# Second mixer's softmax steps: row maxima ahead of finished heads, evacuation of transposes ahead of squares and conversions, first output products inside the last steps

## The reference

```python
q = (rms_norm(cq, qa_g) @ w_uq).reshape(B, S, MLA_HEADS, MLA_QK)          # 6 heads of 128 + 64
kv = (rms_norm(ckv, kva_g) @ w_ukv).reshape(B, S, MLA_HEADS, MLA_NOPE + MLA_VDIM)
...
q = rms_norm(q, qn_g)
k = rms_norm(k, kn_g)
... # rotary on the last 64 of q and k; then, per block of 128 queries:
s = jnp.einsum('bqhd,bkhd->bhqk', qi, k).astype(jnp.float32) * scale
s = jnp.where(kpos[None, :] <= qpos[:, None], s, -jnp.inf)
p = jax.nn.softmax(s, axis=-1)
return jnp.einsum('bhqk,bkhd->bqhd', p.astype(v.dtype), v)
...
m = memory_attention(z[..., -MEM_W:], rms_norm(mem, mem_norm_g[layer]), w_mem_kv[layer],
                     mem_q_norm_g[layer], mem_k_norm_g[layer])            # 4 heads, 256 memory tokens
x = x + jnp.concatenate([y, m], axis=-1) @ w_out[layer]                   # y: 6 heads of 128, m: 256
x = x + conv_ffn(rms_norm(x, ffn_norm_g[layer]), w_up[layer], ...)
```

## Time and profile before

| | us |
|---|---|
| median of 3 runs (lowest, highest) | 1961.98 (1960.8, 1971.39) |
| the profiled execution | 1967.27 |
| its span | 1965.3 |
| TensorE busy | 1861.8 (95%) |
| VectorE busy | 901.7 (46%) |
| ScalarE busy | 737.6 (38%) |
| GpSimd busy | 725.4 (37%) |
| mean granted TensorE clock | 0.971 |

### The profile page before, as it was taken

The page is one execution under the profiler, slowest core; times in us unless marked ns, Lnnn a source line. Parts: engine busy times, 40 slices in busy tenths (PEclk is TensorE's granted clock), DMA queues, the critical chain, the costliest instruction groups (busy, mean ns, idle before and its releaser), DMA issues.

```text
span 1965.3 us, 24503 instructions
## 1 busy us (share of the span) xinstructions
PE 1861.8 (95%) x9553; PEld 1496.6 (76%) x9553; DVE 901.7 (46%) x1293; ACT 737.6 (38%) x977; POOL 725.4 (37%) x226
## 2 busy tenths in 40 slices
PE   7999979999999999988899999998899999999998
PEld 5799754788888887565788888886787778878876
DVE  5245754356554116555355555104516734413453
ACT  4142143355545224453345455223213542221323
POOL 2253820334443444221144444343324434343321
PEclk8989996999999999999999999999999999999999
DMA  6632110222222232110122222223131112322121
GB/s 258 253 107 87 44 44 1 72 100 88 104 101 79 88 97 95 42 65 22 43 88 104 99 93 87 88 88 121 65 84 45 55 65 86 120 88 105 65 86 43
DMA packets 28663, 170.30 MB, mean 87 GB/s; under 512 B 2992, under 2 KB 5296, under 8 KB 12208
## 3 DMA queue, kind: packets, MB, share of 16 engines
q1 hardware_dynamic: 25200, 151.20, 22.3%
q10 hardware_dynamic: 3392, 18.09, 2.8%
HBM read 167.18 MB, written 2.10 MB: 86 GB/s over the span
## 4 chain that ended last, share of the span: by engine, by line
PE 66%; issue 17%; DVE 7%; POOL 7%; ACT 3%; DMA 0%; POOLq 0%; ACTq 0%; DVEq 0%
PE ps L390 40%; PE ps L714 11%; POOL wlo L1035 5%; POOL hk L1061 1%; PE ps L408 1%; PE ps L409 1%; PE ps L410 1%; DVE scr L2063 1%; PE ps L956 1%; PE ps L805 1%; PE ps L966 1%; PE ps L939 1%; PE ps L967 1%; PE ps L968 1%; PE ps L687 1%
## 5 line engine op out<-in xcount | busy, mean ns | idle before, releaser
L1035 POOL TENSOR_TENSOR wlo<-wraw,whi 128x2048 fp32r<-128x2048 f32 (+3 forms) x153 | 650.1, 4249 | 1112.0 <-ACT whi L1151 1094.1
L390 PE MATMUL ps<-hh,whi 128*128 128x512 f32 x1344 | 527.4, 392 | 2.3 <-DVE sig L2233 1.6
L390 PE MATMUL ps<-hl,whi 128*128 128x512 f32 x1344 | 523.1, 389 | 0.0
L390 PE MATMUL ps<-hh,wlo 128*128 128x512 f32 x1344 | 523.1, 389 | 0.0
L1151 ACT ACTIVATE whi<-wraw 128x2048 fp32r<-128x2048 f32 (+3 forms) x149 | 265.0, 1779 | 416.0 <-PE ps L390 326.1
L390 PEld LDWEIGHTS ps<-hh,whi 128*128 128x128 f32 x1344 | 252.3, 188 | 58.9 <-issue 3.6
L390 PEld LDWEIGHTS ps<-hh,wlo 128*128 128x128 f32 x1344 | 252.3, 188 | 53.0
L390 PEld LDWEIGHTS ps<-hl,whi 128*128 128x128 f32 x1344 | 252.4, 188 | 52.5 <-issue 1.2
L1900 DVE SCALAR_TENSOR_TENSOR scr<-ps,vec,scr 128x510 f32<-128x510 f32 (+1 forms) x176 | 120.2, 744 | 93.2 <-ACT scr L1344 93.2
L714 PE MATMUL ps<-gh,whi 128*128 128x512 f32 x352 | 137.1, 390 | 1.3 <-DVE gl L1915 1.3
L714 PE MATMUL ps<-gh,wlo 128*128 128x512 f32 x352 | 137.0, 389 | 0.0
(11 more groups left out here) (432 smaller groups left out, 2857.0 us busy)
## 6 DMA issues: line engine op xcount, KB each, us to landing
wraw<-in_w SPq DMA_DIRECT2D x63, 1024.0 KB, 4.9
wraw<-in_w0b SPq DMA_DIRECT2D x26, 1024.0 KB, 4.8
wraw<-in_w1o SPq DMA_DIRECT2D x26, 1024.0 KB, 4.9
wraw<-in_wd SPq DMA_DIRECT2D x32, 704.0 KB, 4.1
ada<-in_wada ACTq DMA_DIRECT2D x12, 1024.0 KB, 7.1
xtok<-in_x SPq DMA_DIRECT2D x4, 512.0 KB, 7.9
out<-ytok SPq DMA_DIRECT2D x2, 1024.0 KB, 4.2
wraw<-in_w SPq DMA_DIRECT2D x3, 576.0 KB, 3.9
```

The source lines that it names most:

```text
L390: last = mm(o, l, r, start=(k == 0 and n == 0), stop=(k == K - 1 and n == 2))
L1035: nc.gpsimd.tensor_tensor(wlo[:, s % 2, 0:wd], wraw[:, s % 2, 0:wd], whi[:, s % 2, 0:wd].bitcast(F32), ALU.subtract).then_inc(lo_ready, 1)
```

## The change

On VectorE the row maxima of a pass come ahead of the finished head. Both heads of a pair are copied together, ahead of the normalisation, and the low part of the second one is taken in the next pass. On ScalarE the squares and conversions move behind the evacuation of the transposes; the values' evacuation and job 8 stay ahead of it. TensorE does 36 of the 48 products of output slot 0 in passes 17 to 20, between transposes and scores, and 12 products of slot 1 before the last 12 of slot 0. Slot 1 no longer waits for slot 0's addition. Slots 2 and 3 are as they were. GpSimd and SyncE have the lists that they had.

```diff
@@ TensorE
+            Y_ORDER = (6, 7, 0, 1, 2, 3, 4, 5)
+            def out_part(s, j0, j1):
+                for j in range(j0, j1):
+                    k = Y_ORDER[j]
+                    pe.wait_ge(split_done, Q_Y1 + j + 1)
+                    for b in range(2):
+                        o, w_ = ps[:, 2 * (s % 2) + b, :], wv(s % 2, 256, off=b * P)
+                        mm(o, w_(0, k), y_act(0, k), start=(j == 0), stop=False)
+                        mm(o, w_(0, k), y_act(1, k), start=False, stop=False)
+                        last = mm(o, w_(1, k), y_act(0, k), start=False, stop=(j == 7))
+                return last
...
+                if n >= 17:
+                    if n == 17:
+                        pe.wait_ge(m_ev, taken(2, 11))
+                        pe.wait_ge(lo_ready, S_O1 + 1)
+                    out_part(S_O1, *((0, 2), (2, 4), (4, 5), (5, 6))[n - 17])
                 if n < 19:
                     pe.wait_ge(g_ex, 2 * n + 2)
...
                     step_pv(n - 1).then_inc(g_pv, 1)
-            out_slots(S_O1, Q_Y1, act=lambda a, k: (oh1, ol1)[a][:, k, :] if k < 6 else (ohm, olm)[a][:, k - 6, :],
-                      order=(6, 7, 0, 1, 2, 3, 4, 5))
+            pe.wait_ge(g_ex, 40)
+            pe.wait_ge(lo_ready, S_O1 + 2)
+            out_part(S_O1 + 1, 0, 2)
+            out_part(S_O1, 6, 8).then_inc(used, 1)
+            out_part(S_O1 + 1, 2, 8).then_inc(used, 1)
+            pe.wait_ge(emptied, S_O1 + 1)
+            pe.wait_ge(lo_ready, S_O1 + 3)
+            plain(S_O1 % 2, y_act).then_inc(used, 1)
...
@@ ScalarE
-            def job(pr, k):
+            def squares_and_weights(pr, k):
                 if k < 5:
...
                     A(sqt[:, k, :], x, ACT.Square).then_inc(m_sq, 1)
-                    if k == 2:
-                        conv_upto(S_UQ + 2 * pr + 2)
-                elif k < 7:
+                if k == 2:
+                    conv_upto(S_UQ + 2 * pr + 2)
+                elif k == 6:
+                    conv_upto(S_UQ + 2 * pr + 3)
+
+            def job(pr, k):
+                if k in (5, 6):
...
-                    if k == 6:
-                        conv_upto(S_UQ + 2 * pr + 3)
...
+                if n in (13, 17, 21):
+                    hi(oh1[:, 2 * (n // 4 - 3), :])
+                if n < 20:
                     for pr, k in JOBS[n + 1]:
                         job(pr, k)
                 if 1 <= n < 21:
...
                         A(ptm[:, e, 0:nch, :], ps[:, 4 + e, 0:nch * P].rearrange("p (c t) -> p c t", t=P), ACT.Copy).then_inc(g_pt, 1)
+                if n < 20:
+                    for pr, k in JOBS[n + 1]:
+                        squares_and_weights(pr, k)
                 if n in (5, 9):
                     hi(ohm[:, n // 4 - 1, :])
                 elif n in (13, 17, 21):
-                    for e in range(2):
-                        hi(oh1[:, 2 * (n // 4 - 3) + e, :])
-            act.wait_ge(v_ev, 6)
-            act.sem_inc(emptied, 3)
+                    hi(oh1[:, 2 * (n // 4 - 3) + 1, :])
+                if n == 16:
+                    act.wait_ge(v_ev, 6)
+                    act.sem_inc(emptied, 3)
...
@@ VectorE
-            for n in range(22):
-                if n in (5, 9):
-                    hp = n // 4 - 1
-                    dve.wait_ge(g_pv, n - 1)
-                    split(lambda t: copy(t, ps[:, 6 + hp, :]), ohm[:, hp, :], olm[:, hp, :])
-                elif n in (13, 17, 21):
-                    dve.wait_ge(g_pv, n - 1)
-                    take_head(2 * (n // 4 - 3))
-                if n >= 20:
-                    continue
+            for n in range(20):
                 wd, c = chunks(n) * P, 2 * (n % 2)
                 dve.wait_ge(g_sc, n + 1)
...
+                if n in (5, 9):
+                    hp = n // 4 - 1
+                    dve.wait_ge(g_pv, n - 1)
+                    split(lambda t: copy(t, ps[:, 6 + hp, :]), ohm[:, hp, :], olm[:, hp, :])
+                elif n in (13, 17):
+                    dve.wait_ge(g_pv, n - 1)
+                    take_head(2 * (n // 4 - 3))
+                    take_head(2 * (n // 4 - 3) + 1)
+                elif n == 18:
+                    flush()
...
-                if n in (13, 17):
-                    take_head(2 * (n // 4 - 3) + 1)
+            dve.wait_ge(g_pv, 20)
+            take_head(4)
             take_head(5)
             flush()
```

More of the change, by code:

```diff
@@ L842, in _, with y_act @@
             last.then_inc(tok_mm, 1)
+            Y_ORDER = (6, 7, 0, 1, 2, 3, 4, 5)
+            def y_act(a, k):
+                return (oh1, ol1)[a][:, k, :] if k < 6 else (ohm, olm)[a][:, k - 6, :]
+            def out_part(s, j0, j1):
[8 more added lines that the diff above has]
+                return last
             for n in range(21):
@@ L863, in _ @@
                     step_pv(n - 1).then_inc(g_pv, 1)
-            out_slots(S_O1, Q_Y1, act=lambda a, k: (oh1, ol1)[a][:, k, :] if k < 6 else (ohm, olm)[a][:, k - 6, :],
-                      order=(6, 7, 0, 1, 2, 3, 4, 5))
+            pe.wait_ge(g_ex, 40)
[6 more added lines that the diff above has]
+            plain(S_O1 % 2, y_act).then_inc(used, 1)
+            pe.wait_ge(emptied, S_O1 + 2)
+            pe.wait_ge(lo_ready, S_O1 + 4)
+            for b in range(2):
+                three(ps[:, 2 * ((S_O1 + 3) % 2) + b, :], wv((S_O1 + 3) % 2, 256, off=b * P),
+                      y_act, 8).then_inc((half_used, used)[b], 1)
             ffn(S_U1, S_D1, 1)
@@ L1440, in _ @@
             for pr, k in JOBS[0]:
-                job(pr, k)
+                squares_and_weights(pr, k)
             for n in range(22):
```

## The result

| | before | after |
|---|---|---|
| median, us (lowest to highest, 4 runs each) | 1961.94 (1960.8 to 1971.39) | 1941.22 (1939.13 to 1944.7) |
| ratio, 95% interval | | 0.9879 (0.9851 to 0.9907) |
| the same kernel once more, 5 runs against 9 of before | 1967.6 | 1939.87, ratio 0.9855 (0.9832 to 0.9879) |
| span of the profiled execution | 1965.3 | 1937.2 |
| TensorE busy in it | 1861.8 (95%) | 1851.9 (96%) |

Faster by 20.7 us between the medians of the first sets and by 27.7 between those of the second; 1943 was forecast. The two traces differ by 28.1 us, and the first thing to find is where these lie.

What follows compares the result with a forecast made beforehand. TensorE, busy 95% of the span, was taken as the bound, its waits mostly ending on ScalarE. Savings of 4.3 + 0.9 + 2.0 + 11.8 = 19.0 us off the 1961.98 median gave 1943; 8-in-10 range 1936 to 1953.

Steps and rivals of the forecast that it cites:

- Part 1: ScalarE evacuates transposes ahead of squares and conversions: 4.3 us in steps 1 to 7, 0.9 net at step 11.
- The 0.9 left at steps 1 and 2: TensorE's waits for evacuated transposes at steps 1 and 2, of which about 0.9 us each was expected to stay.
- the price at step 11: Slot 0's later conversion delays GpSimd's pass, which holds VectorE's row-maximum scaling: 1.3 us charged against 2.2 gained.
- Step 13: Row maximum ahead of a head's copy and low part: 1.2 us, plus 1.7 of clock, less 0.9 at scores 15.
- The 1.7 of clock: At step 13, a TensorE wait cut to some 0.3 us keeps the clock up from 896 to 900: 1.7 us.
- Part 3: Output products moved into steps 17 to 20 and slot 1 begun early fill TensorE's idle time: 11.8 us gained.
- the restarts: TensorE switching between product shapes when output products are laid between steps: 0.1 us each, four, 0.4 charged.
- The maximum at pass 17: VectorE's row maximum comes 1.2 us earlier; 12 output products cover the rest of TensorE's 3.20 us wait.
- part 2: VectorE takes row maxima ahead of finished heads; 2.0 us net at step 13, nothing extra at steps 5 and 9.
- Only the end gains: Rival: VectorE, held by GpSimd's passes, gives back the earlier savings; only 11.8 us remain, 1950 us; chance 17%.
- Slot 2 as the bound: Rival: slot 2's output weights come 3 us later, costing 1.3 us at slots 2 and 3: 1946 us; chance 6%.
- the lasting fall of the clock: Rival: mixed products lower the granted clock through the output slots, each product costing 0.23 us more: 1987 us; chance 3%.

Runs made afterwards that it cites:

- e3: Kernel before with only the row maxima moved ahead of the finished heads on VectorE: 1959.63 us against 1968.64.
- e2: Kernel before with only the evacuation of transposes moved ahead of squares and conversions on ScalarE: 1962.08 us against 1968.64.
- e7: Changed kernel with output slot 0's conversion in pass 10 put back ahead of the evacuation of transposes: 1940.16 us against 1969.97 for the kernel before.
- e4: Kernel before with the ScalarE and VectorE reorderings but TensorE's old list: 1956.52 us against 1968.64; run once more, 1955.21.
- e6: Changed kernel with slot 0's 36 products all behind the loop, slot 1 still early: 1949.9 us against 1969.97 for the kernel before; once more, 1946.34.
- e5: Changed kernel with slot 0's 36 products laid 12, 6, 12, 6 over passes 17 to 20: 1943.07 us against 1969.97 for the kernel before.
- e8: Changed kernel with the row-maximum scaling as two 128x1 instructions with a scalar operand from SBUF: 1943.59 us against 1969.97 for the kernel before.
- e9: Changed kernel with output products re-laid from pass 15, evacuations earlier in passes 1 and 2, split scaling at step 11: 1938.36 us against 1967.6 for kernel before.

## Why the prediction was right, and where it was off

The mechanism was right in the main: each of the three parts shortens TensorE's path at the places named, and each was measured alone. The sizes of the terms were less good, and the last step, from the sum to a time, was helped by luck.

- **Where the bound lies: right.** A microsecond off TensorE's path in the stage came off the end, the output slots behind it stayed full, and slot 2's weights were ready 1.3 us ahead (1.7 forecast).
- **Part 1: 5.2 forecast, 6.2 measured** (step 10's values 80.9 us after the rotary product before, 883.45 - 802.57, and 74.7 after, 875.08 - 800.37). Two things make the difference. I counted nothing for the maximum ahead of the memory heads, and e3 shows 0.8 by then, with a wait of 0.63 for VectorE gone. And in e2, without that, the gain by then is 5.7: 0.5 more than the brackets removed. Over the whole stage part 1 alone is worth 5.0. The 0.9 left at steps 1 and 2 is there (0.89 twice), and so is the price at step 11: scaling 3.21 (about 3.4 forecast), wait 1.26 (1.3 forecast). Its reason, the later conversion, was mostly wrong, as e7 shows: the pass came late with the square.
- **Step 13, 2.0 forecast: 2.4** (to step 15's values). Left over are 0.21 and 1.00, where I had 0.3 and 1.3. The 1.7 of clock in it came, but not by the reason given. The wait before scores 14 is 0.20 in e4 too, and there the clock fell at 100 us in one execution and at 93 in the other. A shorter wait at step 13 did not keep it up.
- **Part 3, 11.8 forecast: 13.4** (50.80 against 37.40 in the last rows of the two tables). Idle time went from 11.4 to 0.8 as forecast; the wait of 0.8 at step 18's values came as 0.83. What was wrong is the restarts, charged at 0.4, for which the prediction shows no row. Busy time fell too, from 39.44 to 36.57: 1.7 of it is the clock, and 1.2 is what the waits cost beside their brackets. I read that as the product before a wait running out alone (0.39 long, where the next one starts after 0.23) and the one behind it starting slowly (0.33 to the next); the profile models the ends of products, so only the sum is measured.
- **The maximum at pass 17, "1.2 earlier": wrong in size, 3.2**, as e3 and e6 show. It did no harm to the sum, since the products would have filled the rest; it hid how much part 2 is worth alone.
- **The sum: 19.0 forecast, 21.9 in the stage.** It was added up for the stage, 2.9 too low. Nothing was forecast for the part behind the stage, where some 4 us went as well.
- **The time: partly luck.** I subtracted 19.0 from the median shown, 1961.98, and got 1943 against 1941.22. That median was low: three other sets of the kernel before have 1967.6 to 1969.97, while the changed kernel has 1939.87 the second time. Counted from 1967.6 the forecast would have been 1948.6, 8.7 too high.
- **The rivals.** "Only the end gains" falls by e2 and e4. Slot 2 as the bound and the lasting fall of the clock did not come.
- **Still open: the clock.** 3.4 us of the sum were forecast for two falls that would go, and they went. In the eight profiles with early slot 1 and parts 1 and 2 (after twice, e5, e6 twice, e7, e8, e9) the stage ran at 1.00; in all six others it fell. But e4 and e6 have the same list for TensorE up to the loop's end, and one fell there and the other did not. Whether filling keeps the clock up, as I assumed, is not settled: e6 kept it without filling. It is worth up to 3.4 us of the 21.9, and one late fall makes most of the 4 us behind.

## What to carry to other kernels

Look at what an engine's queue holds ahead of the instruction that the bottleneck waits for, and move there only what no one needs soon; then follow the moved work to the next engine that shares something with the one on the path (here square, rotary product, low-part pass, scaling). A copy ahead of a short critical instruction costs its own wait too, not only its duration. Work of the next stage whose operands are done can fill the waits of a chain, if its banks are free; and an edit of a few microseconds is judged in its own stage, not by the span alone. Then the unchanged parts are laid beside each other over several kernels, since here one of them went with the edit.

## What the runs showed of the hardware that I had not expected

- Unchanged instructions took another time at another granted clock, and it went with what stood ahead of them: the part behind the stage took 985.08 and 985.13 us in the changed kernel, 989.03 before and 988.10 in e9.
- One kernel's clock differs between executions: e4's stage ran at 0.98 and at 0.96. The median of before was 1961.94, 1968.64, 1969.97 and 1967.6 in four sets of runs; no run says how much of that is the clock.
- VectorE's instruction on 128x2 numbers was held for 3 us by GpSimd's pass; two on 128x1 with a scalar operand from SBUF were not held at all, but a pair of that form on 128x128 was (5.80 us instead of 0.48).
- Removing a wait of TensorE gives more than the wait: at an equal clock, 1.2 us over the five fewer waits from step 15's values to slot 2.
